# A decoder trunk in fp32 on one core: two conv tiles on TensorE instead of three, tap products added by accumulating DMA

## What is computed

```python
proj = h @ w_in + b_in                       # 512 x 6144: value, gate, z
val, glu_gate, z = jnp.split(proj, 3, axis=-1)
u = val * jax.nn.sigmoid(glu_gate)           # 512 x 2048
u = lax.conv_general_dilated(u, conv_w[:, None, :], window_strides=(1,),
    padding=[(CONV_KERNEL - 1, 0)], feature_group_count=CONV_WIDTH, ...) + conv_b   # 31 taps, depthwise, causal
u = jax.nn.silu(layer_norm(u, norm_g, norm_b))   # over the 2048 channels
u = u * jax.nn.silu(z)
return u @ w_out + b_out
```

## Time and profile before

| | |
|---|---|
| median of 3 runs | 799.83 us (798.99 to 800.45) |
| the profiled execution | 798.19 us, of which its span 796.4 us |
| PE busy | 785.1 us, 99% of the span, 3803 matmuls |
| DVE, POOL, ACT busy | 585.6, 530.0, 392.5 us |
| transfers | 111.35 MB, the DMA engines busy in 47.3% of the span |
| granted TensorE clock | 0.998 |

### The profile page before, as it was taken

One profiled execution on the slowest core, in us unless ns is written; L12 is line 12 of the kernel. 1 busy time (PEld: TensorE's weight loads), 2 busy tenths in 40 slices (PEclk: granted clock), 3 DMA queues, 4 the chain that ended last, 5 costly groups with the idle time before them and its releaser, 6 DMA issues.

```text
span 796.4 us, 11156 instructions
## 1 busy us (share of the span) xinstructions
PE 785.1 (99%) x3803; PEld 664.1 (83%) x3803; DVE 585.6 (74%) x1006; ACT 392.5 (49%) x687; POOL 530.0 (67%) x324
## 2 busy tenths in 40 slices
PE   8999999999999999999999999999999999999996
PEld 7888888888888878888988888888888888878885
DVE  2699999999999879975633480158778988866217
ACT  5465564553634577421333443267676766564110
POOL 4689997996987763872564367157777766477430
PEclk9999999999999999999999999999999999999999
DMA  6333466565544325541334326236666674663412
GB/s 227 106 106 107 129 180 189 129 185 142 158 135 115 96 80 171 200 131 54 106 106 119 87 73 172 66 113 192 178 191 197 188 218 128 190 203 110 159 52 105
DMA packets 130030, 111.35 MB, mean 140 GB/s; under 512 B 16986, under 2 KB 109248, under 8 KB 129980
## 3 DMA queue, kind: packets, MB, share of 16 engines
q1 hardware_dynamic: 129980, 110.72, 47.3%
HBM read 88.85 MB, written 14.25 MB: 129 GB/s over the span
## 4 chain that ended last, share of the span: by engine, by line
PE 94%; DVE 2%; DMA 1%; issue 1%; POOL 1%; SPq 0%; ACT 0%; DVEq 0%; ACTq 0%
PE bank L1878 88%; PE bank L2190 1%; PE bank L2191 1%; DMA x_in<-in_x_dram 1%; DVE acc L1556 1%; PE bank L1968 1%; PE bank L1965 1%; PE bank L1966 1%; POOL pt_lo L975 1%; DVE bank L1563 0%; DMA prob_moved<-prob_kept 0%; PE bank L2063 0%; PE bank L2183 0%; POOL w_lo L823 0%; PE bank L2181 0%
## 5 line engine op out<-in xcount | busy, mean ns | idle before, releaser
L823 POOL TENSOR_TENSOR w_lo<-w_raw,w_hi 128x1024 fp32r<-128x1024 f32 x102 | 253.9, 2498 | 122.7 <-ACT w_hi L1016 115.1
L1473 DVE SCALAR_TENSOR_TENSOR bank<-u,conv_w,bank 128x512 f32<-128x512 f32 x291 | 193.6, 748 | 0.0
L1016 ACT ACTIVATE w_hi<-w_raw 128x1024 fp32r<-128x1024 f32 x102 | 107.4, 1057 | 107.1 <-DMA w_raw<-in_a_w_in_dram 42.4
L1878 PE MATMUL bank<-xt_hi,w_lo 128*128 128x512 f32 (+1 forms) x392 | 152.1, 388 | 0.0
L1878 PE MATMUL bank<-xt_hi,w_hi 128*128 128x512 f32 (+1 forms) x392 | 150.9, 385 | 0.0
L1878 PE MATMUL bank<-xt_lo,w_hi 128*128 128x512 f32 (+1 forms) x392 | 150.8, 385 | 0.0
L1878 PEld LDWEIGHTS bank<-xt_lo,w_hi 128*128 128x128 f32 x392 | 73.7, 188 | 15.1 <-issue 0.5
L1878 PEld LDWEIGHTS bank<-xt_hi,w_lo 128*128 128x128 f32 x392 | 73.7, 188 | 15.0 <-issue 0.5
L1878 PEld LDWEIGHTS bank<-xt_hi,w_hi 128*128 128x128 f32 x392 | 73.6, 188 | 14.8
L1878 PE MATMUL bank<-ht_hi,w_lo 128*128 128x512 f32 (+1 forms) x208 | 76.0, 365 | 0.0
L1878 PE MATMUL bank<-ht_lo,w_hi 128*128 128x512 f32 (+1 forms) x208 | 75.8, 365 | 0.0
(11 more groups left out here) (228 smaller groups left out, 1725.8 us busy)
## 6 DMA issues: line engine op xcount, KB each, us to landing
w_raw<-in_a_w_in_dram SPq DMA_DIRECT2D x48, 512.0 KB, 3.9
w_raw<-in_b_w_in_dram SPq DMA_DIRECT2D x20, 512.0 KB, 3.6
prob_kept<-prob SPq DMA_DIRECT2D x16, 640.0 KB, 3.5
prob_moved<-prob_kept SPq DMA_DIRECT2D x64, 160.0 KB, 3.2
w_raw<-in_a_w_out_dram SPq DMA_DIRECT2D x16, 512.0 KB, 4.1
w_raw<-in_b_w_out_dram SPq DMA_DIRECT2D x16, 512.0 KB, 3.6
stacked<-u_kept SPq DMA_DIRECT2D x48, 132.0 KB, 4.1
bundle_raw<-in_b_w_uq_dram SPq DMA_DIRECT2D x16, 256.0 KB, 4.3
```

The costliest lines, as they stand in the source:

```text
L823: nc.gpsimd.tensor_tensor(w_lo[slot][:], w_raw[raw][:], w_hi[slot][:].bitcast(F32), ALU.subtract).then_inc(w_lo_ready, 1)
L1016: nc.scalar.activation(w_hi[slot][:], w_raw[raw][:], ACT.Copy).then_inc(w_hi_ready, 1)
L1473: nc.vector.scalar_tensor_tensor(out=inner[:] if k < TAPS - 1 else acc[:, t, :], in0=u[:, t, k:k + SEQ], scalar=conv_w[:, column:column + ...
L1878: last = nc.tensor.matmul(out_ap, a, b, start=(start and n == 0 and m == 0), stop=(stop and n == len(parts) - 1 and m == 2))
```

## The change

Tile 4 leaves TensorE's packs: `MATRIX_TILES` becomes (8, 12), with eight packs instead of twelve. It becomes the late tile, 22 taps as products by ACT and additions by POOL, 9 taps on DVE. Tile 11 becomes a whole tile of DVE, and tile 7 leaves DVE. Tiles 1 and 7 are "grouped": ACT writes four products at a time as one block of four tiles (1 MB), and POOL no longer adds them itself but issues a DMA from its own queue that adds the block onto a block of four sums (`accum_op=ALU.add`): six such transfers for tile 1, five for tile 7, one in each pair 4 to 9 and 11 to 15. POOL adds the four sums of a tile at the end (`sum_group`, three instructions) and the last taps one by one (3 of tile 1, 7 of tile 7). The blocks lie in tiles 8 to 15 of `acc`, in z_a and in the first tiles of `u`, all of them free at that time; new waits guard this. ACT copies a pack behind the value of the pair instead of behind the products. POOL's sum over channels begins at z chunk 7 instead of 6.

```diff
+        second_sums = at("second_sums", reg_u, 0, [P, 4, SEQ])
...
-        MATRIX_ROWS = (1, 2, 3)
+        MATRIX_ROWS = (2, 3)
         MATRIX_TILES = tuple(MATRIX_COLUMN + CT // TAP_ROWS * row for row in MATRIX_ROWS)
-        BEGINS = (6, 10, 14)
-        PACKS_AT = (17, 25, 35)
+        BEGINS = (10, 14)
+        PACKS_AT = (26, 35)
         PACK_BANK = 6
         PART_SHIFT = SHIFTS
-        PART_TILES = ((0, 2, 3), (5, 6, 7))
+        PART_TILES = (5, 6, 9)
...
-        LATE_TILE, LATE_TAPS = 11, 17
-        SHARED_TILES = (1,)
-        VECTOR_TILES = (0, 2, 3, 5, 6, 7, 9, 10, 13, 14, 15, LATE_TILE)
-        shared_taps = [(t, k) for t in SHARED_TILES for k in range(TAPS)] + [(LATE_TILE, k) for k in range(LATE_TAPS)]
-        BEFORE_GATING = 3
-        PAIR_SHARE = {3: 3, 4: 4, 5: 2, 6: 3, 7: 4, 8: 3, 9: 4, 10: 3, 11: 1, 12: 4, 13: 4, 14: 3, 15: 1}
-        Z_SHARE = {0: 1, 1: 2, 2: 2, 3: 2, 4: 2}
...
+        GROUPED_TILES = (1, 7)
+        LATE_TILE, LATE_TAPS = 4, 22
+        VECTOR_TILES = (0, 2, 3, 5, 6, 9, 10, 11, 13, 14, 15, LATE_TILE)
+        GROUP = 4
+        FIRST_GROUPS, SECOND_GROUPS = 6, 5
+        GROUP_PAIRS = (4, 5, 6, 7, 8, 9, 11, 12, 13, 14, 15)
+        GROUPED_TAPS = (GROUP * (FIRST_GROUPS + 1), GROUP * (SECOND_GROUPS + 1))
+        def taps_of(t, first, n):
+            return [(t, k) for k in range(first, first + n)]
+        BEFORE_GATING, AFTER_GATING, IN_Z = {}, {}, {}
+        EARLIER, LATER = GROUPED_TILES
+        BEFORE_GATING[3] = taps_of(EARLIER, 0, GROUP)
+        for g, t in enumerate(GROUP_PAIRS):
+            BEFORE_GATING[t] = (taps_of(EARLIER, GROUP * (g + 1), GROUP) if g < FIRST_GROUPS else
+                                taps_of(LATER, GROUP * (g + 1 - FIRST_GROUPS), GROUP))
+        BEFORE_GATING[10] = taps_of(EARLIER, GROUPED_TAPS[0], TAPS - GROUPED_TAPS[0])
+        AFTER_GATING[10] = taps_of(LATER, 0, GROUP)
+        first = 0
+        for t, n in ((6, 3), (7, 2), (8, 2), (9, 3), (12, 3), (13, 4), (14, 2), (15, 1)):
+            AFTER_GATING[t] = taps_of(LATE_TILE, first, n)
+            first += n
+        IN_Z[1] = taps_of(LATE_TILE, first, LATE_TAPS - first)
+        first = GROUPED_TAPS[1]
+        for i, n in ((4, 2), (5, 2), (6, 2), (7, 1)):
+            IN_Z[i] = taps_of(LATER, first, n)
+            first += n
+        shared_taps = [tap for t in range(CT) for half in (BEFORE_GATING, AFTER_GATING) for tap in half.get(t, ())]
+        shared_taps += [tap for i in range(CT) for tap in IN_Z.get(i, ())]
+        def apart(t, k):
+            return t in GROUPED_TILES and k < GROUPED_TAPS[GROUPED_TILES.index(t)]
+        def added(t, k):
+            return k > 0 and not apart(t, k)
...
+        def group_sums(t):
+            return acc[:, CT - GROUP:, :] if t == EARLIER else second_sums
+        def group_products(g):
+            if g in (7, 9):
+                return acc[:, CT - GROUP:, :]
+            if g in (1, 3, 5):
+                return acc[:, CT - 2 * GROUP:CT - GROUP, :]
+            return z_a[:, 1:1 + GROUP, :]
...
-        POOL_SUM_BEGINS = 6
-        POOL_SUM = (1, 0, 2, 3, 5, 6, 7, 9, 10, 4, 13, 14, 8, 15)
+        POOL_SUM_BEGINS = 7
+        POOL_SUM = (1, 0, 2, 3, 5, 6, 9, 10, 11, 13, 8, 14, 7, 15)
         HALF_TAPS = 16
-        PARTS_AFTER = {7: 0, 13: 1, LATE_TILE: 2}
...
+        PARTS_AFTER = {13: 0, LATE_TILE: 1}
...
+                    if g == q == 0:
+                        sp.wait_ge(group_added, 16 * (FIRST_GROUPS if m == 0 else 10))
...
-                for n in pair_taps(t)[:BEFORE_GATING]:
-                    add_product(n)
+                if t == GROUP_PAIRS[FIRST_GROUPS]:
+                    sum_group(0)
+                if t == GROUP_PAIRS[FIRST_GROUPS] + 1:
+                    add_products(BEFORE_GATING[10])
+                add_products(AFTER_GATING.get(t - 1, ()))
                 if t > 0:
                     glu(t - 1, (t - 1) % 2)
+                if t in GROUP_PAIRS:
+                    add_group(GROUP_PAIRS.index(t))
...
+            def add_group(g):
+                t, k = BEFORE_GATING[GROUP_PAIRS[g]][-1]
+                pool.wait_ge(product_ready, shared_taps.index((t, k)) + 1)
+                wait(pool, group_added, 16 * g)
+                nc.gpsimd.dma_start(group_sums(t)[:], group_products(g)[:], accum_op=ALU.add).then_inc(group_added, 16)
+            def sum_group(which):
+                t = GROUPED_TILES[which]
+                pool.wait_ge(group_added, 16 * (FIRST_GROUPS + which * SECOND_GROUPS))
+                for n in range(1, GROUP):
+                    if n > 1:
+                        pool.wait_ge(group_summed, (GROUP - 1) * which + n - 1)
+                    nc.gpsimd.tensor_tensor(acc[:, t, :], group_sums(t)[:, 0, :] if n == 1 else acc[:, t, :],
+                                            group_sums(t)[:, n, :], ALU.add).then_inc(group_summed, 1)
+            def add_products(taps):
+                for t, k in taps:
+                    if not added(t, k):
+                        continue
+                    if t in GROUPED_TILES:
+                        pool.wait_ge(group_summed, (GROUP - 1) * (GROUPED_TILES.index(t) + 1))
+                    pool.wait_ge(product_ready, shared_taps.index((t, k)) + 1)
+                    wait(pool, product_added, added_up_to((t, k)) - 1)
+                    nc.gpsimd.tensor_tensor(acc[:, t, :], acc[:, t, :], tap_product[added_up_to((t, k)) % 4][:], ALU.add
+                                            ).then_inc(product_added, 1)
...
             for i in range(CT):
+                if 2 * (i - POOL_SUM_BEGINS) + 2 >= len(POOL_SUM) - 1:
+                    sum_tiles(2 * (i - POOL_SUM_BEGINS))
                 if i != 1:
                     split_lo(Z0 + i, i % 2, i % SLOTS)
                 if i == 0:
                     split_lo(Z0 + 1, 1, 1)
+                    add_products(AFTER_GATING[CT - 1])
                     glu(CT - 1, (CT - 1) % 2)
-                for n in z_taps(i):
-                    add_product(n)
-                if i >= POOL_SUM_BEGINS:
+                if i == 3:
+                    sum_group(1)
+                add_products(IN_Z.get(i, ()))
+                if 0 <= 2 * (i - POOL_SUM_BEGINS) < len(POOL_SUM) - 3:
                     sum_tiles(2 * (i - POOL_SUM_BEGINS))
...
                 keep_value(t - 1, (t - 1) % ROUND)
-                for n in pair_taps(t)[:BEFORE_GATING + 1]:
-                    tap_times_u(n)
-                if t in PARTS_START_IN_PAIR:
-                    start_parts(PARTS_START_IN_PAIR[t])
+                keep_pack_after(2 * t - 2)
+                for tap in BEFORE_GATING.get(t, ()):
+                    tap_times_u(*tap)
                 if t in START_BEFORE_GATING:
                     start_chains(START_BEFORE_GATING[t])
-                keep_pack_after(2 * t - 2)
                 keep_gate_half(t - 1, (t - 1) % ROUND)
                 if t in BEGINS:
                     conv_input_hi(BEGINS.index(t))
-                for n in pair_taps(t)[BEFORE_GATING + 1:]:
-                    tap_times_u(n)
+                for tap in AFTER_GATING.get(t, ()):
+                    tap_times_u(*tap)
...
+                if apart(t, k) and k < GROUP:
+                    if t == LATER and k == 0:
+                        act.wait_ge(tap_done, whole_at()[3])
+                        act.wait_ge(product_ready, shared_taps.index((t, k)))
+                    out = group_sums(t)[:, k, :]
+                elif apart(t, k):
+                    g = k // GROUP - 1 + FIRST_GROUPS * GROUPED_TILES.index(t)
+                    wait(act, group_added, 16 * (g - 1))
+                    if g == 7:
+                        act.wait_ge(group_summed, GROUP - 1)
+                    out = group_products(g)[:, k % GROUP, :]
...
+                if i == 1:
+                    act.wait_ge(group_added, 16 * len(GROUP_PAIRS))
...
+                    if t in (9, 13) and k == TAPS - 1:
+                        dve.wait_ge(group_added, 16 * (FIRST_GROUPS if t == 9 else 10))
```

More of the change, by code:

```diff
@@ L228, in trunk_kernel @@
         part_out = [at(f"part_out{i}", cos_at, i * TILE, [P, SEQ]) for i in range(2)]
-        u_kept = [nc.dram_tensor(f"u_kept{m}", [2, P, SEQ + PAD], F32).ap() for m in range(3)]
+        u_kept = [nc.dram_tensor(f"u_kept{m}", [2, P, SEQ + PAD], F32).ap() for m in range(2)]
         z_a = at("z_a", reg_z, 0, [P, CT, SEQ])
@@ L422, in added_before @@
-        def added_before(n):
-            return sum(1 for _, k in shared_taps[:n] if k > 0)
+        GROUPED_TILES = (1, 7)
[7 more added lines that the diff above has]
+            return [(t, k) for k in range(first, first + n)]
@@ new lines, in trunk_kernel, with added_up_to @@
+        shared_taps += [tap for i in range(CT) for tap in IN_Z.get(i, ())]
[3 more added lines that the diff above has]
+            return k > 0 and not apart(t, k)
+        def added_up_to(tap):
+            return sum(1 for t, k in shared_taps[:shared_taps.index(tap) + 1] if added(t, k))
```

(26 more changed lines are left out.)

45 lines of the change are left out of this document (19 added, 26 removed).

## The result

The changed kernel takes 802.70 us in the median of 6 runs (800.79 to 804.21), the kernel before 799.24 in the same session. The ratio is 1.0044, 95% interval 1.003 to 1.0058: slower by 0.44%, where 0.9935 was forecast. One rival had the sign and nearly the time (802.4), but not the mechanism, so that its number fits by luck.

The account below looks back on a forecast made before the run. TensorE and VectorE were taken to reach the mean over channels together, so the slower sets it: TensorE gains 5.5 us, VectorE 5.2, and 799.83 - 5.2 = 794.6 us. Its own range was 794.0 to 796.5, the wider one 793.8 to 801.5.

Parts of the forecast that it names:

- TensorE's and VectorE's terms: Ahead of the mean over channels: four packs fewer save TensorE 5.5 us; five taps and one add_parts fewer save VectorE 5.2.
- the sum of 5.2: The mean over channels comes 5.2 us earlier, set by VectorE, giving 794.6 us.
- D, the issue on GpSimd: GpSimd's time to issue one transfer, taken as 1.0 us; up to 1.7 it costs nothing at chunk 26.
- The accumulating transfer, 8 us: Landing time of 1 MB added onto SBUF, taken as 8 us, hidden under the 10.9 between issues.
- rival of the slow transfers: Landings beyond 10.9 us stall GpSimd in pairs 5 to 9, 12 and 13; at 13 us, 802.4; chance 0.20.
- crowded weight loads: Rival: new transfers delay w_raw's loads; at 9 us six pairs lose 1.6 each, 798.7, no change; chance 0.12.
- The limit that the text set, a landing of 7.4: Weight load, w_hi 1.07 and w_lo 2.4 must fit in 10.9 us, so loads may land in 7.4, not 3.9.
- ScalarE's cover in pair 10: ScalarE starts tile 9's chains at about 125 us, VectorE needs them at 129.2: covered by some 4 us.
- GpSimd's channel sum: GpSimd's sum over channels ends at 259.4 us, needed at 260.7: covered by 1.3.
- The forecast's own range: 794.0 to 796.5 us, from L1484's cost varying and 0.9 for a chain that starts late; chance 0.50.
- From the mean to the end: After the mean over channels, an early mean was taken to shift all that follows, so 5.2 us counted in full.

Follow-up runs that it names:

- five profiles: Changed kernel with all eleven or late five accumulating transfers cut to 64 KB, late five cut with old scratch, halved, or not adding: 0.9961, 0.9956, 0.994, 0.9959, 0.996.
- late-sliver run: Changed kernel with only the five late accumulating transfers (pairs 11 to 15) cut to 64 KB each, their products left out: 0.9956 of the kernel before.
- slivers: Changed kernel with accumulating transfers cut from 1 MB to 64 KB, issues and waits kept: all eleven 0.9961, late five 0.9956 of the kernel before.
- halves: Changed kernel with the five late accumulating transfers moving only two of their four blocks, half of those products left out: 0.9959 of the kernel before.
- copies: Changed kernel with the five late transfers writing their 1 MB without adding: 0.996 of the kernel before.
- two last versions: Changed kernel, last transfer in z chunk 1 from z_a, first stacks early, packs copied before splits: 0.9989; also second stacks a chunk later: 0.9973 of the kernel before.
- all sixteen: The profiles of all changed kernels, the changed one and its follow-up variants; their ratios to the kernel before run from 0.994 to 1.0056.

## Why the prediction was wrong

- **TensorE's and VectorE's terms, the sum of 5.2: right.** With the crowding gone the mean came 5.26, 5.26, 5.28, 5.27 and 5.25 earlier in five profiles, at 262.0 to 263.1 on the clock, and `csum` stood ready at 261.87 in the late-sliver run (261.4 forecast).
- **D, the issue on GpSimd: right.** 0.85 to 0.88 us in ten of the eleven issues and 1.05 in the first, for 1.0.
- **The accumulating transfer, 8 us: right as a latency.** 6.9 to 8.1 for the ones up to 130 us, 7.0 to 10.7 for the late ones, under 10.9. GpSimd never waits for one before it issues the next, so the rival of the slow transfers, which had the time that came, was wrong in its mechanism.
- **The failed step is the one on crowded weight loads.** The text gave it 0.12 and 4.1 us, six pairs at 1.6, "Against: pieces of only half of each pair overlap". It asked how long one load would take and not whether all the transfers of a stretch fit. They hardly do: the share of the engines before was 0.61 in 150 to 200 us; four transfers at 5.6 in these 50 us are 0.45 more, together 1.06. In 50 to 100 us 0.41 and as much again fit (measured 0.77, in part since the third matrix tile's transfers are gone), and nothing stopped. The slivers (share 0.65), halves (0.82) and copies (0.84) give all of it back, 0.98 gives 7.4 us of stalls. Between them the mean share is no sharp measure: the two last versions have 0.90 and 0.85 with 1.2 and 1.4 us of stalls, the run with the pack's copy in its old place 0.89 with 5.98. It was three stalls, not six pairs of 1.6, and one of them had the lower clock behind it. The limit that the text set, a landing of 7.4, was passed (up to 10.8), and the late issue on SP came on top.
- **How it reached TensorE** was not in the text at all: it let a late load count only where the split missed its chunk. ScalarE also carries the pack's copy behind that wait.
- **The margins**: ScalarE's cover in pair 10 held (VectorE never waited there). GpSimd's channel sum, forecast 1.3 ahead, was not waited for with the slivers and by 0.2 us in the two last versions; in the changed kernel VectorE waits 3.8 for it, since GpSimd stood for late blocks too, but TensorE came no earlier than that. L1567, the former L1484, was put at anything from 0.9 less to 1.0 more than 1.59: it took 1.65 in the changed kernel, 1.66 to 1.73 in the five profiles without stalls and 1.18 to 2.25 over all sixteen, the longest in the two last versions. The forecast's own range was slightly off by itself: with TensorE's 5.5 as the bound it ends at 794.3 and not 794.0.
- **From the mean to the end** the text took one for one. In the five runs without stalls it was 5.3 for 3.2 to 4.3 in the medians; in four of them TensorE's wait on the latent load above is 1.2 to 1.3 of it, and in the halves there is none, so the rest is open. The sum was too large by this, even without the crowding.

The Trainium skill (Collectives: The Full Stack, The bandwidth ceiling) was weighed only for the length of one transfer. Its second read is what the run with copies shows: 5.6 us of the engines against 2.9. Counted over the stretch too, as in the sum of 1.06 above, it would have spoken against the change.

## What to carry to other kernels

A transfer has two prices: until it lands, and how long it holds the DMA engines. Hide the first, but add up the second over each stretch: the share of before plus what is new times the engine time of one. Near 1 (here a sum of 1.06, 0.98 measured) something landed late, whatever its own margin; at 0.84 nothing did that mattered, and in the versions from 0.85 to 0.95 TensorE stood for 1.2 to 6.0 us. Then ask what is queued in order behind the engine that waits for it, since this and not the late data may be what stops the kernel. Bytes that can wait should go where the share is low; here one of eleven transfers, issued 14 us later, took two of the three stalls away.

## What the runs showed of the hardware

- An accumulating transfer of 1 MB, SBUF to SBUF in float32, holds the 16 engines for 5.6 us; in the changed kernel it landed in 6.9 to 8.1 before 130 us and in 7.0 to 10.7 where the loads were late; without the addition 2.9 and 4.5 to 7.3 (median 4.7). The issue takes GpSimd 0.87 in the median with it and 0.58 without.
- At a share of 0.98 a weight load of 512 KB landed in up to 10.8 us (7.2 in the kernel before), and four `stacked` issues on the SP queue took 4.8 and 5.8 us together, where 2.0 is usual. That is not a matter of this share alone: one such group took 3.6 in the kernel before, near 97 us.
- After a stall of 2.2 to 2.3 us TensorE ran some nine matmuls at the lower pace in two profiles (granted clock 0.51 from 169.0 to 172.5 us in the changed kernel); after stalls of 2.1 to 2.9 it did not in five others; after 5.98 it did (0.50 from 172 to 176 us).
